# Reordering the first block of a two-block network in float32 on one core: branch gates between the halves of a recurrence, convolution taps across tiles, layer norm beside an output product

## The reference, cut to what matters

```python
h = rmsnorm(x, norm1_g)
z = h @ w_in + b_in                       # 1024 -> 2048 + 1280 + 1280 + 1024 + 1024
z_glu, z_rx, z_rg, z_ga, z_gb = split(z)
u = z_glu[..., :1024] * sigmoid(z_glu[..., 1024:])
u = causal_depthwise_conv(u, conv_dw_w, conv_dw_b)          # 31 taps
u = silu(layernorm(u, conv_ln_g, conv_ln_b))
y_a = u @ conv_w_out + conv_b_out
xb = causal_depthwise_conv(z_rx, lru_conv_w, lru_conv_b)    # 4 taps
r, i = sigmoid(xb @ wa + ba), sigmoid(xb @ wx + bx)         # block diagonal
a = exp(-8 * r * softplus(-lam))
hb = scan over positions of h = a * h + sqrt(1 - a*a) * (i * xb)
y_b = (hb * gelu(z_rg)) @ lru_w_out
x = x + (sigmoid(z_ga) * y_a + sigmoid(z_gb) * y_b) @ w_mix_out
x = x + swiglu(rmsnorm(x, norm2_g))
x = rmsnorm(x, norm_f_g)
```

## Time and profile before

| | |
|---|---|
| median of 3 runs | 2481.88 us (2481.48 to 2482.76) |
| the profiled execution | 2479.68 us |
| its span | 2477.9 us |
| PE matmul busy | 2344.4 us, 95% |
| DVE, ACT, POOL busy | 38%, 37%, 42% |
| memory traffic | 108 GB/s over the span |

### The profile page before, as it was taken

The page is one execution under the profiler, slowest core; times in us unless marked ns, Lnnn a source line. Parts: engine busy times, 40 slices in busy tenths (PEclk is TensorE's granted clock), DMA queues, the critical chain, the costliest instruction groups (busy, mean ns, idle before and its releaser), DMA issues.

```text
span 2477.9 us, 33699 instructions
## 1 busy us (share of the span) xinstructions
PE 2344.4 (95%) x10556; PEld 1908.0 (77%) x10556; DVE 949.6 (38%) x1601; ACT 926.2 (37%) x1626; POOL 1039.6 (42%) x796
## 2 busy tenths in 40 slices
PE   7999988899999998999997999999999997999997
PEld 6888866778888887888886777777677786888886
DVE  5599967425513314100114044444433344110012
ACT  4333375234422223332333443334343343442331
POOL 4455445344444443444453343332112253554443
PEclk9999999999999999999997999999999997999998
DMA  4333432437737432333331233224111331333331
GB/s 147 97 98 110 120 132 85 148 102 268 261 124 236 154 90 72 97 97 95 95 95 51 81 102 96 95 90 157 43 39 43 119 93 43 102 95 100 98 94 60
DMA packets 130562, 267.98 MB, mean 108 GB/s; under 512 B 14352, under 2 KB 14480, under 8 KB 129712
## 3 DMA queue, kind: packets, MB, share of 16 engines
q1 hardware_dynamic: 119520, 236.51, 31.2%
q10 hardware_dynamic: 10960, 30.38, 3.2%
HBM read 252.12 MB, written 14.68 MB: 108 GB/s over the span
## 4 chain that ended last, share of the span: by engine, by line
PE 82%; issue 7%; DVE 6%; POOL 3%; ACT 2%; DMA 0%; DVEq 0%; ACTq 0%; POOLq 0%
PE bank L856 24%; PE bank L858 23%; PE bank L857 23%; POOL wlo L375 2%; PE bank L1141 2%; PE bank L1199 1%; PE bank L1056 1%; PE bank L1058 1%; PE bank L1057 1%; PE bank L1107 1%; PE bank L1142 1%; PE bank L1125 1%; PE bank L1187 1%; DVE tmp L1513 1%; PE bank L966 1%
## 5 line engine op out<-in xcount | busy, mean ns | idle before, releaser
L375 POOL TENSOR_TENSOR wlo<-raw,whi 128x512 fp32r<-128x512 f32 x750 | 985.4, 1321 | 1335.0 <-ACT whi L447 1334.1
L856 PE MATMUL bank<-a_hi,whi 128*128 128x512 f32 x1992 | 793.8, 398 | 19.5 <-DVE a_lo L1267 7.4
L858 PE MATMUL bank<-a_lo,whi 128*128 128x512 f32 x1992 | 781.4, 392 | 0.0
L857 PE MATMUL bank<-a_hi,wlo 128*128 128x512 f32 x1992 | 781.0, 392 | 0.0
L447 ACT ACTIVATE whi<-raw 128x512 fp32r<-128x512 f32 x750 | 466.7, 627 | 774.1 <-PE bank L858 652.0
L856 PEld LDWEIGHTS bank<-a_hi,whi 128*128 128x128 f32 x1992 | 376.9, 189 | 114.3 <-issue 18.9
L858 PEld LDWEIGHTS bank<-a_lo,whi 128*128 128x128 f32 x1992 | 377.1, 189 | 80.1
L857 PEld LDWEIGHTS bank<-a_hi,wlo 128*128 128x128 f32 x1992 | 377.8, 190 | 74.5
L856 PE MATMUL bank<-b_hi,whi 128*128 128x512 f32 x788 | 313.8, 398 | 24.6 <-POOL wlo L375 9.0
L857 PE MATMUL bank<-b_hi,wlo 128*128 128x512 f32 x788 | 310.3, 394 | 0.0
L858 PE MATMUL bank<-b_lo,whi 128*128 128x512 f32 x788 | 310.3, 394 | 0.0
(11 more groups left out here) (234 smaller groups left out, 1869.2 us busy)
## 6 DMA issues: line engine op xcount, KB each, us to landing
raw<-d_stream SPq DMA_DIRECT2D x750, 256.0 KB, 2.6
G<-d_ada SPq DMA_DIRECT2D x72, 512.0 KB, 4.6
spill_rv<-tmp ACTq DMA_DIRECT2D x32, 256.0 KB, 2.1
G<-spill_rv ACTq DMA_DIRECT2D x6, 1024.0 KB, 9.9
G<-d_x ACTq DMA_DIRECT2D x4, 512.0 KB, 5.4
spill_ga<-G ACTq DMA_DIRECT2D x8, 256.0 KB, 3.6
spill_gb<-G ACTq DMA_DIRECT2D x8, 256.0 KB, 3.6
G<-spill_ga ACTq DMA_DIRECT2D x1, 2048.0 KB, 8.3
```

The source lines that it names most:

```text
L375: pool.tensor_tensor(wlo[:, s % SRING, :], raw[:, s % RING, :], whi[:, s % SRING, :].bitcast(F32), ALU.subtract).then_inc(lo_done, 1)
L856: pe.matmul(out_ps, w_hi, hi[:, k, :], start=first and q == 0, stop=False)
L857: pe.matmul(out_ps, w_lo, hi[:, k, :], start=False, stop=False)
L858: mm = pe.matmul(out_ps, w_hi, lo[:, k, :], start=False, stop=last and q == len(ks) - 1)
```

## The change

In the first block the weights for z_ga and z_gb leave `win` (now 72 panels) and become stages of their own, `ga` after `gates0` and `gb` after `gates1`; the two halves of conv_w_out become one stage `convo` behind `lruo`. The stream in memory keeps its layout; SP reads it in the new order through `LIES`. `gb`'s sigmoids stay on chip, in the place of recurrence tiles that are used up. DVE makes 5 taps after an even gated unit and 18 after an odd one, across tile limits, finishes five tiles before `lru_conv`, and sets tile 5 before the first half's `lru_input`, tile 6 before the first half's scans, and tile 7 behind the second half's scans. `lru_variance` and `lru_scan` write their intermediate to PSUM. The layer norm's sums and broadcasts move into `lruo`: the mean behind its tile 1, the broadcast behind tile 2, the squares behind tile 4, the second broadcast behind tile 5. The mixed operand for `mix` goes through `b_hi` and `b_lo`.

At the norms PE gets matmuls of ones by ones into bank 7 that nobody reads (`keep_warm`), before the statistics, before a broadcast and behind it. The first turn of each wide stage behind a norm (`first_turn`) goes over input tile 0 of all four outputs, then input tile 1 of all four, then tiles 2 and 3 of each; for this ACT rounds the fourth panel before the norm's first operand tile, and the next three between the last ones. The first norm's pairs are added by DVE instead of POOL, and the small set-up operations of DVE move ahead of that norm.

```diff
-    order = [("win", 104, 52), ("gates0", 10, 10), ("convo0", 8, 4), ("gates1", 10, 10), ("convo1", 8, 4),
-             ("lruo", k_panels(KR, KD), KD), ("mix", 16, 8)] + ffn(1) + ffn(2)
+    order = [("win", 72, 36), ("gates0", 10, 10), ("ga", 16, 8), ("gates1", 10, 10), ("gb", 16, 8),
+             ("lruo", k_panels(KR, KD), KD), ("convo", 16, 8), ("mix", 16, 8)] + ffn(1) + ffn(2)
...
-        IG = tiles(S0 + 5 * T, 2)
-        AR = tiles(S0 + 7 * T, 2)
-        STG = tiles(S0, 2)
-        GA = tiles(0, KD)
+        GA = tiles(S0, KD)
         GB = tiles(XR0, KD)
         Y = tiles(0, KD)
-        A5 = [AR[:, 0, :], AR[:, 1, :], G[:, KD * T:(KD + 1) * T], sq[:, 0, :], sq[:, 1, :]]
...
+        A5 = [G[:, S0 + j * T:S0 + (j + 1) * T] for j in (6, 7, 8)] + [XR[:, KR, LPAD:X_ST], a5[:, :]]
+        IG = [AUX[:, :], BCAST[:, :], G[:, S0 + 5 * T:S0 + 6 * T], sq[:, 0, :], sq[:, 1, :]]
+        SQUARED, SCANNED = bank[6][:, :], bank[7][:, :]
...
-                    for k in range(1, KD - 1):
-                        to = PLAN[stage][0] + 8 * (k + 4)
+                    for k, to in zip(range(1, KD - 1), (32, 42, 52, 62, PLAN["ga"][0] + 6, PLAN["gb"][0] - 5)):
...
+            def round_a(fill, val, shift=None, name=None):
+

                 for k in range(KD):
+                    if k in (0, 5, 6, 7):
+                        tick(name, 0, max(k - 4, 0), 1)
                     act.wait_ge(a_val, val + k + 1)
                     if shift is None:
                         act.activation(a_hi[:, k, :], tmp[:, k % 2, :], ACT.Copy).then_inc(a_hi_w, 1)
...
+            wait_evac(act, "win", 0, 14)
+            lru_gates(0)
+            lru_decay(0, (0, 1))
+            tick("ga", 0, 0, 1)
+            lru_decay(0, (2, 3))
+            tick("ga", 0, 1, 1)
+            lru_decay(0, (4,))
+            tick("ga", 0, 2, 3)
+            for j in range(4):
+                first_gate(0, j)
...
             lru_root(0)
-            tick("convo0", 0, 4)
-            tick("convo0", 0, 6)
+            tick("ga", 1, 1, 4)
+            for j in range(4):
+                first_gate(1, j)
+                if j < 3:
+                    tick("ga", 1, 5 + j, 1)
+
             lru_gates(1)
...
             lru_root(1)
-            tick("convo1", 0, 4)
...
-            for m in range(KD):
-                packed_tick("lruo", m, KR)
-                act.wait_ge(a_val, 16 + m + 1)
-                act.activation(a_hi[:, m, :], tmp[:, m % 2, :], ACT.Copy).then_inc(a_hi_w, 1)
+            tick("gb", 0, 4, 1)
+            for j in range(4):
+                second_gate(0, j)
+                if j < 3:
+                    tick("gb", 0, 5 + j, 1)
+            tick("gb", 1, 0, 5)
+            for j in range(4):
+                second_gate(1, j)
+                if j < 3:
+                    tick("gb", 1, 5 + j, 1)
...
+            for s in range(k_panels(KR, KD)):
+                tick("lruo", 0, s, 1)
+                if s == 1:
+                    for j in range(2):
+                        act.wait_ge(stage_out[j], 16 * KD // 2)
+                    act.wait_ge(opb, FILL_B["yb"] + KR)
+                    act.dma_start(GA[:, :, :], spill_ga).then_inc(ld_ga, 16)
+                    act.dma_start(X[:, :, :], xT).then_inc(ld_x2, 16)
+                if s == 9:
+                    for k in range(KD):
+                        act.wait_ge(centred, k + 1)
+                        square(NORM["ln"], k, U[:, k, PAD:U_ST])
+                for k in {15: (0,), 16: (1,), 17: (2, 3), 18: (4,), 19: (5, 6, 7)}.get(s, ()):
+                    act.wait_ge(a_val, 8 + k + 1)
+                    act.activation(tmp[:, k % 2, :], tmp[:, k % 2, :], ACT.Silu, bias=col("conv_ln_b", k)).then_inc(u_silu, 1)
...
+            def first_turn(name, ops, ready, fill, beside=None):
+
+
+                for k in range(2):
+                    for j in range(4):
+                        if k == 0:
+                            bank_free(name, 0, j)
+                        panel(name, 0, j, (k,), bank_of(name, j)[:, :], ops, k == 0, False, q0=k, done=False,
+                              ready=(ready, fill) if j == 0 else None)
+                for j in range(4):
+                    panel(name, 0, j, (2, 3), bank_of(name, j)[:, :], ops, False, False, q0=2,
+                          ready=(ready, fill) if j == 0 else None)
+                wide_turn(name, 0, ops, ready, fill, (1,))
...
+            def keep_warm(n):
+
+
+                for _ in range(n):
+                    pe.matmul(bank[7][:, 0:P], ones[:, :], ones[:, :], start=True, stop=True)
...
+
+
+                keep_warm(warm)
...
-            pe.wait_ge(conv_done, KD)
-            sum_tile(KD - 1, U[:, KD - 1, PAD:U_ST], mean_summed)
-            win_turn(11, (0,))
-            broadcast(2)
-            win_turn(11, (1,))
...
             lru_gates(0)
-            for m in range(4):
-                tile8("convo0", 0, m, OPA, opa, FILL_A["u2"], m == 0)
+            for i in range(2):
+                wide_turn("ga", i, OPA, opa, FILL_A["h1"])
             lru_gates(1)
-            for m in range(4):
-                tile8("convo1", 0, m, OPA, opa, FILL_A["u2"], False)
+            for i in range(2):
+                wide_turn("gb", i, OPA, opa, FILL_A["h1"])
             for m in range(KD):
                 tile_packed("lruo", m, KR, OPB, opb, FILL_B["yb"])
+                if m == 1:
+                    pe.wait_ge(conv_added, KD - 2)
+                    sum_tile(0, SQ_ACC, None)
+                    pe.wait_ge(conv_done, KD)
+                    sum_tile(KD - 1, U[:, KD - 1, PAD:U_ST], mean_summed)
+                if m == 2:
+                    pe.wait_ge(ix_done, KR)
+                    broadcast(2)
+                if m == 4:
+                    for k in range(KD):
+                        sum_square(NORM["ln"], k)
+                if m == 5:
+                    broadcast(3)
             for m in range(KD):
-                tile8("mix", 0, m, OPA, opa, FILL_A["mix"], m == 0)
+                tile8("convo", 0, m, OPA, opa, FILL_A["u2"], m == 0)
+            for m in range(KD):
+                tile8("mix", 0, m, OPB, opb, FILL_B["mix"], m == 0)
...
-            broadcast(4)
+            broadcast(4, warm=8)
+            keep_warm(10)
...
-            norm_stat(NORM["n1"])
-            operand_a("h1", lambda k: col("norm1_g", k))
+            for j in range(4):
+                dve.wait_ge(sq_ready, 2 * j + 2)
+                dve.tensor_tensor(SQ_FIRST[:, 2 * j, :], SQ_FIRST[:, 2 * j, :], SQ_FIRST[:, 2 * j + 1, :], ALU.add).then_inc(pair_ready, 1)
...
+            norm_stat(NORM["n1"])
+            operand_a("h1", lambda k: col("norm1_g", k))
...
+            def conv_run(lo, hi):
...
+                for m in range(lo // TAPS, -(-hi // TAPS)):
+                    conv_taps(m, max(lo - m * TAPS, 0), min(hi - m * TAPS, TAPS))
+
+
+            taps = 0
+            for m in range(KD):
+                i, j = m // 2, m % 2
+                dve.wait_ge(evac[2 * j + 1], i + 2)
+                dve.scalar_tensor_tensor(out=U[:, m + 1, PAD:U_ST], in0=bank[2 * j][:, :], scalar=col("b_in", 2 * m),
+                                         in1=R5[:, j, :], op0=ALU.add, op1=ALU.mult).then_inc(evac[2 * j], 1)
+                dve.wait_ge(evac[2 * j], i + 2)
+                more = 5 * TAPS if m == KD - 1 else taps + (18 if j else 5)
+                conv_run(taps, more)
+                taps = more
...
+            for m in range(KR):
+                lru_conv(m)
+            conv_taps(5, 0, TAPS)
+            lru_input(0)
+            lru_variance(0)
+            conv_taps(6, 0, TAPS)
+            lru_scan(0)
+            lru_input(1)
+            lru_variance(1)
+            lru_scan(1)
+            filled["b"] = FILL_B["yb"] + KR
+            conv_taps(7, 0, TAPS)
+
+            def gate_recurrent(m):
...
+            gate_recurrent(0)
+            dve.wait_ge(mean_summed, 1)
+            dve.tensor_scalar(small[:, 1, 0:4], AUX[:, 0:4], 1.0 / D, None, ALU.mult).then_inc(st_ready, 1)
+            stat[0] += 1
+            gate_recurrent(1)
+            dve.wait_ge(bc_ready, stat[0])
+            for k in range(KD):
+                dve.tensor_tensor(U[:, k, PAD:U_ST], U[:, k, PAD:U_ST], BCAST[:, :], ALU.subtract).then_inc(centred, 1)
+            gate_recurrent(2)
+            gate_recurrent(3)
             norm_stat(NORM["ln"])
             for k in range(KD + 1):
...
             filled["a"] = FILL_A["u2"] + KD
+            gate_recurrent(6)
+            gate_recurrent(7)
...
+            dve.wait_ge(ld_ga, 16)
...
+                        dve.wait_ge(opb, FILL_B["mix"] + m - 1)
+                    wait_used(dve, "convo", 0, 2 * m + 1)
+                    dve.scalar_tensor_tensor(out=tmp[:, m % 2, :], in0=bank_of("convo", m)[:, :], scalar=col("conv_b_out", m),
+                                             in1=GA[:, m, :], op0=ALU.add, op1=ALU.mult).then_inc(evac_of("convo", m), 1)
```

(5 more changed lines are left out.)

363 lines of the change are left out of this document (162 added, 201 removed).

## The result

| | before | after |
|---|---|---|
| median | 2482.32 us (2481.48 to 2487.90, 4 runs) | 2452.14 us (2447.25 to 2454.84, 4 runs) |
| ratio | | 0.9865, 95% interval 0.985 to 0.988 |
| profiled execution, its span | 2479.68, 2477.9 us | 2453.66, 2451.5 us |

What follows compares the result with a forecast made beforehand. PE was taken as the bound, losing 45.9 us from `gates0` to the end of `mix`. Block 34 plus norms 15 made 49, so profiled execution 2479.68 - 49 = 2431 and median about 2432 us, range 2416 to 2453.

Steps and rivals of the forecast that it cites:

- gain 34 forecast: First block: about 12 us of stalls (7.6 + 2 + 2 + 0.5) in place of 45.9.
- The walk along DVE: First block: DVE's joints at 220.6, 276.5, 303.5, 316.7, 343.7 and 365.2 us, with scans of 5.4 each.
- one stall left, at the mean: In `lruo` behind two tiles: PE waits 7.6 us for tile 7 of taps, and some 2 for the clock.
- the entry of `convo`: Start of `convo`: the layer norm's silus come late in `lruo`, a stall of 2 us (0 to 6).
- a sign of being wrong: In `gb` or `gates1`: PE waiting for ACT, its sigmoids held by lru_done, would show the forecast wrong.
- 15 forecast: All norms: earlier statistics, the first turn's order and dummies for the clock bring 15 us, bounds 0 and 20.
- The price per first turn: Behind norms: twelve matmuls take 5.5 us where 2.72 would do; 3.2 lost at the first norm, 2.8 behind `mix`.
- let them start earlier; I put 1.7: First norm: pairs on DVE and setup moved ahead start the statistics 1.7 us earlier, bounds 0 and 3.
- Rival 1: First block: DVE later than walked, scans at 6.5 to 7.7 or slower taps; time 2442 to 2465, chance 0.20.
- Rival 2: Norms: dummies leave the clock at 0.50 or delay the broadcast; gain 34, time 2446 (2438 to 2452), chance 0.11.
- Rival 3: First block and norms: scans at 3.8, no stall at `lruo`, gain 41 + 20, time below 2418; chance 0.03.
- Rival 4: First block: slower, DVE's chain to tile 7's end grows by 49 us or more; time 2485 to 2500, chance 0.06.

Runs made afterwards that it cites:

- the block alone: The changed kernel with the norms as before (no dummies, old first turn, late roundings, first norm's pairs on POOL): 2454.46 us, 0.9874 to before.
- the kernel with early additions: The change with the first norm's additions on DVE ahead of the wait for the column and constant loads: 2450.12 us, 0.9855 to before.

## Why the prediction was right in kind and too large

**The block: gain 34 forecast, 25.1 shown** (by the block alone). The walk along DVE was right to 2 us at each of six joints, over 145 us, and so was the picture of one stall left, at the mean; it was 3.12, not 7.6, because PE came 2.7 later, DVE 0.9 sooner, and eight sums of 0.95 in all stand ahead of the wait. `lruo` lost 22.1 with the block alone, where the forecast has 7.6 + 2 and the layer norm's sums that stay (14.4 less 3.2 of the first turn), 20.8. That these two are so close is luck: the stall with its clock was 3.3 us smaller than forecast, and the sums of squares 4.9 larger. Before, the 64 one-column products stood in four groups of 16 between turns of `win`, at granted clock 1.00, and each group put off the next product by 1.8 us, 7.2 in all:

```profile
292.67 1.84 PE L913 MATMUL bank<-ones,sq 128*128 128x1 f32 x16
```

In the change they stand in one row behind tile 4 of `lruo` and cost 12.1, of which 2.2 are products at low clock behind them. The prediction took the cost over unchanged. No run puts them back into groups.

So the mis-sized terms are three: these sums; the entry of `convo`, "2 (0 to 6)", which cost 6.9 with the block alone and 6.5 in the change (the wait of 4.00 and low clock behind it); and `gb`, costed at nothing, which lost 2.0. The prediction gave the sigmoids that wait for lru_done "3 or more" us to spare and named PE waiting in `gb` for them as a sign of being wrong. In this small form the sign came: ACT was held for 2.73 (the row of 302.45) and PE for 1.22. The 8.9 us between 34 and 25.1 are 4.9 at `convo`, 2.0 in `gb`, 1.3 in `lruo` and 0.7 of small ones.

**The norms: 15 forecast, next to nothing net.** The price per first turn was right. The first 12 products took 2.84 or 2.85 at all five norms (5.51 and 5.05 to 5.15 before), and the first 48 took 11.0 in place of 13.5 to 14.9, 15.8 us in all five. What failed is that this was taken for the sum. First, "let them start earlier; I put 1.7" for the first norm: they started 2.2 later. The additions were moved to DVE behind a wait for `cols`, which POOL had never had; the step that reads every wait ahead of a moved instruction was not made. And without that wait it was still 0.2 sooner only, for the small instructions beside POOL. Second, the dummies do delay: 0.5 at n2, 0.4 and 0.6 further on. Behind `mix` the broadcast came 4.2 us after the last sums instead of 2.9:

```profile
522.51 1.26 PE L1027 MATMUL bank<-consts,small 128*128 128x128 f32 x8
...
526.09 0.47 PE L910 MATMUL bank<-a_hi,whi 128*128 128x512 f32 x1
...
553.32 0.54 PE L910 MATMUL bank<-a_hi,whi 128*128 128x512 f32 x1 [2.15 <-POOL wlo L382]
```

Third, the first feed-forward gave back its 3.5: the row of 553.32 is a stall of a turn later, 2.15, with some 2 us at low clock behind it. In the change SP's loads of the modulation's weights lie behind loads of the stream in one queue, DVE waited 3.00 for one of them, ACT for DVE's gated unit and POOL for ACT:

```profile
548.73 1.29 DVE L1376 SCALAR_TENSOR_TENSOR bank<-G,small,bank 128x1024 f32<-128x1024 f32 x1 [3.00 <-DMA G<-d_ada]
```

The new order of the first turn is needed for this stall. All eight kernels with it have it, 0.23 to 2.15 us, each 0.8 to 0.9 less than DVE's wait for that load; the six with the old order don't, though DVE waited up to 3.98 in them. How long the load keeps DVE varies with the same code: 3.00 here and 1.81 in the kernel with early additions, whose ffn1 took 382.9 for 385.6. That the order delays the load through SP's queue is argued. Fourth, the attention took 2.7 more, though its own first turn won 2.5 (last section).

**The rivals.** Rival 1 (DVE later) did not come, but its mechanism is real: without the move of the intermediates to PSUM the kernel is 11 us slower. Rival 2 was half right: the clock was high, the delay was paid. Rival 3 (more than forecast) did not come: the scans took 5.5 us each, not 3.8. Rival 4 was far: tile 7 ended at 364, not 414.

**The range.** 2452 lies in 2416 to 2453 by one microsecond, and that is luck. Its upper part stood for late scans (rival 1, from 2442) or dummies that do not hold the clock (rival 2, 2438 to 2452); the scans were on time and the clock was held. The 24 us that are missing are the terms above.

## What to carry to other kernels

A serial chain that lasts longer than any one stage wants stages between its links that need nothing of it; a walk by instruction durations with its waits predicts its joints to a few us, and the stall at its end can be taken away by moving who asks, as the mean's sums one tile later show. When an instruction changes engine, list the waits that the new engine has already taken in front of it. One-column products in one long row cost more than the same in short groups between wide ones, 12.1 us for 7.2. Small gains in a program with a varying clock are counted by stretches, not by the total, and even a stretch with the same code differed by 2 to 3 us between kernels: five times 3 us were there, and none was left at the end.
